# A recurrent trunk with product-key experts: prompt activations turned, and expert gates built from high and low halves

## The reference, cut to what matters

```
q = x @ w_q                                     # 8 heads, two halves of 128
s1, s2 = q_half1 @ keys1.T, q_half2 @ keys2.T   # 128 scores each
top16 of each, top16 of their 256 sums -> 16 (i, j) per head, gates = softmax
act[t, e] = gelu(x[t] . u[e])
out[t]    = sum over the 128 chosen e = (i, j) of gate * act[t, e] * v[e]
```

## Time and profile before

| | us |
|---|---|
| median of 3 runs | 5470.12 |
| the profiled execution | 5478.42 |
| its span, first to last instruction | 5476.7 |
| TensorE busy in the span | 5146.4 |
| VectorE busy | 2764.4 |
| ScalarE busy | 1416.8 |

### The profile page before, as it was taken

How to read it: one execution, slowest core, us unless ns; L and a number is a source line. 1 busy time by engine, 2 the same in 40 slices (tenths; PEclk the granted TensorE clock), 3 DMA queues, 4 the chain that set the end, 5 groups by cost and what they waited for, 6 DMA issues and landing times.

```text
span 5476.7 us, 70249 instructions
## 1 busy us (share of the span) xinstructions
PE 5146.4 (94%) x30167; PEld 4571.0 (83%) x30167; DVE 2764.4 (50%) x4785; ACT 1416.8 (26%) x1532; POOL 1495.3 (27%) x839
## 2 busy tenths in 40 slices
PE   5999779999999989999799999899999999999997
PEld 3767679999999978888566678889999999878886
DVE  2162668914434056666455541389524342266666
ACT  0110022223444222222222222112234443222222
POOL 0020222332222265542011110123322222465431
PEclk7969999999999999999799999999999999999999
DMA  7141022334444478886210011112334444588873
GB/s 292 63 166 58 20 77 82 121 118 154 154 157 158 164 258 304 303 303 249 84 39 32 31 47 43 47 62 108 123 130 156 155 161 148 198 314 300 296 295 135
DMA packets 295262, 835.85 MB, mean 153 GB/s; under 512 B 23922, under 2 KB 157298, under 8 KB 242726
## 3 DMA queue, kind: packets, MB, share of 16 engines
q1 hardware_dynamic: 91680, 520.91, 25.8%
q10 hardware_dynamic: 158216, 176.07, 9.3%
q0 software_dynamic: 45056, 134.38, 7.1%
HBM read 674.40 MB, written 156.80 MB: 152 GB/s over the span
## 4 chain that ended last, share of the span: by engine, by line
PE 89%; DVE 5%; POOL 2%; ACT 1%; issue 1%; DMA 1%; SPq 0%; DVEq 0%; ACTq 0%; POOLq 0%
PE PS L584 20%; PE PS L585 20%; PE PS L586 20%; PE PS L635 4%; PE PS L706 3%; PE PS L429 3%; PE PS L819 3%; PE PS L797 3%; PE PS L489 3%; PE PS L781 2%; POOL A L1837 1%; PE PS L576 1%; DVE EP L1338 1%; DMA ring<-in_w_mod 1%; PE PS L703 1%
## 5 line engine op out<-in xcount | busy, mean ns | idle before, releaser
L584 PE MATMUL PS<-hH,wH 128*128 128x320 f32 x4608 | 1439.5, 312 | 29.5 <-DVE hL L1106 28.4
L585 PE MATMUL PS<-hL,wH 128*128 128x320 f32 x4608 | 1425.5, 309 | 0.0
L586 PE MATMUL PS<-hH,wL 128*128 128x320 f32 x4608 | 1425.3, 309 | 0.0
L1826 POOL TENSOR_TENSOR wL<-raw,wH 128x2048 fp32r<-128x2048 f32 x144 | 667.9, 4639 | 1660.8 <-ACT wH L1560 1660.8
L584 PEld LDWEIGHTS PS<-hH,wH 128*128 128x128 f32 x4608 | 867.0, 188 | 30.7 <-issue 29.2
L585 PEld LDWEIGHTS PS<-hL,wH 128*128 128x128 f32 x4608 | 867.0, 188 | 0.0
L586 PEld LDWEIGHTS PS<-hH,wL 128*128 128x128 f32 x4608 | 866.2, 188 | 0.0
L1560 ACT ACTIVATE wH<-raw 128x2048 fp32r<-128x2048 f32 x272 | 520.3, 1914 | 1111.9 <-PE PS L586 1052.4
L586 PE MATMUL PS<-wH,WL 128*128 128x512 f32 x2048 | 803.7, 392 | 0.0
L1213 DVE TENSOR_TENSOR wL<-raw,wH 128x2048 fp32r<-128x2048 f32 x128 | 293.3, 2292 | 461.4 <-ACT wH L1560 461.4
L1845 POOL DMA_INDIRECT ubuf<-in_v,idxV x256 | 352.3, 1376 | 579.7 <-DVE acc L1225 536.2
(11 more groups left out here) (331 smaller groups left out, 6566.4 us busy)
## 6 DMA issues: line engine op xcount, KB each, us to landing
raw<-in_u SPq DMA_DIRECT2D x128, 1024.0 KB, 4.8
raw<-in_v SPq DMA_DIRECT2D x128, 1024.0 KB, 4.9
expert_acts<-abuf ACTq DMA_DIRECT2D x128, 640.0 KB, 2.9
expert_gates<-wide ACTq DMA_DIRECT2D x64, 1024.0 KB, 5.1
wide<-expert_acts SPq DMA_DIRECT2D x64, 1024.0 KB, 5.8
ring<-in_w_mod SPq DMA_DIRECT2D x48, 1024.0 KB, 9.0
wide<-expert_gates SPq DMA_DIRECT2D x16, 2048.0 KB, 11.7
gb<-expert_gates SPq DMA_DIRECT2D x16, 2048.0 KB, 12.1
```

The costliest lines, as they stand in the source:

```text
L584: nc.tensor.matmul(out, lhsH, rhsH, start=start, stop=False)
L585: nc.tensor.matmul(out, lhsH, rhsL, start=False, stop=False)
L586: return nc.tensor.matmul(out, lhsL, rhsH, start=False, stop=stop)
L1826: G.tensor_tensor(wL[:, n % NSPLIT, :], raw[:, n % NRAW, :], wH[:, n % NSPLIT, :].bitcast(f32), ALU.subtract).then_inc(lo_u, 1)
```

## The change

**Activations.** In `act_block` only the sample's 512 tokens are still made with the weights of `u` stationary: 8 x 3 = 24 matmuls of 512 columns a block, into one PSUM bank. The prompt's 128 tokens are turned: once a pair, after the second block, the tokens (`hH`, `hL`) are the stationary operand and the 256 experts of the pair the moving one: 24 matmuls of 256 columns into bank 2. They have a gelu, a buffer (`abuf0`) and a tensor in memory (`A0d`, token-major) of their own, stored every four pairs; `Ad` now holds the sample alone. `fetch_act` gathers from `A0d`; the index arithmetic on VectorE gets shorter.

**Gates.** The gates are split in a high and a low half (`gH`, `gP`). The one-hots are `f32r`, and the second is multiplied by either half, so a group has four VectorE operations of 128x1024 instead of three. A build is cut in two, `build(q, 0)` and `build(q, 1)`, of four tokens: four `f32r` matmuls of 256 columns, high and low side by side. The first stands in the middle of the block's 24 products, the second after its end (after the prompt's products, where the block has them). ScalarE copies the high part of four tokens to `gst` (`gate_half`), then VectorE adds the low part from PSUM to it in place (`gates_out`), and only that addition raises `g_evac`.

**The order on VectorE** is now: both one-hot groups 0 and 1, then for each q: addition (q, 0), the two comparisons of group q+1, addition (q, 1), the two multiplications of group q+1.

The core of the diff:

```diff
+    A0d = nc.dram_tensor("prompt_acts", [P, N_KEYS * N_KEYS], f32, kind="Internal").ap()
-    Ad = nc.dram_tensor("expert_acts", [NBLK, P, JB, T], f32, kind="Internal").ap()
+    Ad = nc.dram_tensor("expert_acts", [NBLK, P, JB, DEC], f32, kind="Internal").ap()
-    acts = Ad.rearrange("b p j (t o) -> (b p j t) o", o=1)
+    acts = A0d.rearrange("t (e o) -> (t e) o", o=1)
...
-    hots_ = wide[:, 4096:8192].rearrange("p (s c t n) -> p s c t n", s=2, c=2, t=8)
+    hots_ = wideR[:, 4096:10240].rearrange("p (s c t n) -> p s c t n", s=2, c=3, t=8)
+    gP = PS[:, 5:7, :]
+    gates_ = PS[:, 3:5, :].rearrange("p b (t c j) -> p c (b t) j", t=2, c=2)
...
-                    done(feature_major_split(slot, b % 2, b % 2), ("a", l, b))
+                    for half in range(2):
+                        for k in range(4 * half, 4 * half + 4):
+                            w = slice(k * SLICE + (b % 2) * P, k * SLICE + (b % 2 + 1) * P)
+                            last = split_products(PS[:, b % 2, :], wH[:, slot, w], wL[:, slot, w], hH[:, k, P:T], hL[:, k, P:T],
+                                                  k == 0, k == KD - 1)
+                        if half == 0 and build_group is not None:
+                            build(build_group, 0)
+                    done(last, ("a", l, b))
+                    if b % 2 == 1:
+                        if l * 64 + b // 2 >= 1:
+                            pe.wait_ge(act0_gelu, l * 64 + b // 2)
+                        for k in range(KD):
+                            w = slice(k * SLICE, (k + 1) * SLICE)
+                            last = split_products(PS[:, 2, 0:SLICE], hH[:, k, 0:P], hL[:, k, 0:P], wH[:, slot, w], wL[:, slot, w],
+                                                  k == 0, k == KD - 1)
+                        done(last, ("a0", l, b // 2))
+                    if build_group is not None:
+                        build(build_group, 1)
...
-                def build(q):
-                    pe.wait_ge(hot_ready, l * NGRP + q + 1)
-                    if q:
-                        pe.wait_ge(g_evac, l * NGRP + q)
-                    for tk in range(8):
-                        last = nc.tensor.matmul(PS[:, 4 + tk // 4, (tk % 4) * P:(tk % 4 + 1) * P], hots_[:, q % 2, 0, tk, :],
-                                                hots_[:, q % 2, 1, tk, :], start=True, stop=True)
+                def build(q, c):
+                    if c == 0:
+                        pe.wait_ge(hot_ready, l * NGRP + q + 1)
+                    if q or c:
+                        pe.wait_ge(g_evac, 2 * (l * NGRP + q) + c)
+                    for tk in range(4):
+                        last = nc.tensor.matmul(PS[:, 3 + tk // 2, (tk % 2) * 2 * P:(tk % 2 + 1) * 2 * P].rearrange("p (c j) -> p c j", c=2),
+                                                hots_[:, q % 2, 0, 4 * c + tk, :], hots_[:, q % 2, 1:3, 4 * c + tk, :], start=True, stop=True)
...
+                def gates_out(q, c):
+                    ve.wait_ge(g_high, 2 * (l * NGRP + q) + c + 1)
+                    first = (q % 2) * 8 + 4 * c
+                    out = gst[:, q // 2 % 2, :, first:first + 4].rearrange("p i t -> p t i")
+                    V.tensor_tensor(out, out, gates_[:, 1], ALU.add).then_inc(g_evac, 1)
+
+                for q in range(2):
+                    hots(q, 0)
+                    hots(q, 1)
                 for q in range(NGRP):
-                    hots(q)
+                    gates_out(q, 0)
+                    if 1 <= q < NGRP - 1:
+                        hots(q + 1, 0)
+                    gates_out(q, 1)
+                    if 1 <= q < NGRP - 1:
+                        hots(q + 1, 1)
...
+                def gate_half(q, c):
+                    s, first = q // 2 % 2, (q % 2) * 8 + 4 * c
+                    act.wait_ge(products, at["g", l, q, c])
+                    S.activation(gst[:, s, :, first:first + 4].rearrange("p i t -> p t i"), gates_[:, 0], ACT.Copy).then_inc(g_high, 1)
```

More of the change, by code:

```diff
@@ L249, in trunk @@
     WL1 = sb("WL1", [P, JV, DEC], f32r, scope=pv)
-    sb("v_pad", [P, 82 * KB], scope=pv)
+    sb("v_pad", [P, 80 * KB], scope=pv)
+    acc0 = sb("acc0", [P, D], scope=pv)
+    ubuf0 = sb("ubuf0", [P, D], scope=pv)
     WL0 = sb("WL0", [P, JV, DEC], f32r, scope=pv)
-    acc0 = sb("acc0", [P, D], scope=pv)
-    ubuf = sb("ubuf", [P, NGAT, D], scope=pv)
+    ubuf1 = sb("ubuf1", [P, NGAT - 1, D], scope=pv)
+    ubuf = [ubuf0[:]] + [ubuf1[:, i, :] for i in range(NGAT - 1)]
     pv.close()
@@ new lines, in act_block @@
+                    if build_group is not None:
[8 more added lines that the diff above has]
+                                                hots_[:, q % 2, 0, 4 * c + tk, :], hots_[:, q % 2, 1:3, 4 * c + tk, :], start=True, stop=True)
+                    done(last, ("g", l, q, c))
@@ L1180, in peer @@
                     ve.wait_ge(products, at["hk", l, t])
-                    V.tensor_copy(hkT[:, :, (t - 1) * P:t * P], PS[:, 4 + t % 2, 0:2 * P].rearrange("p (c t) -> p c t", c=2)).then_inc(hk_evac, 1)
+                    V.tensor_copy(hkT[:, :, (t - 1) * P:t * P], PS[:, 3 + t % 2, 0:2 * P].rearrange("p (c t) -> p c t", c=2)).then_inc(hk_evac, 1)
                 ve.wait_ge(hk_evac, l * 4 + 4)
[L1183 to L1187, removed]
+                link(V.tensor_copy(gH[:], gP[:, 0, :]))
@@ L1188, in hots @@
+                link(V.tensor_tensor(gP[:, 1, :], gP[:, 0, :], gH[:].bitcast(f32), ALU.subtract))
+                link(V.tensor_copy(gP[:, 0, :], gH[:].bitcast(f32)))
+                def hots(q, half):
                     ts = slice(8 * q, 8 * q + 8)
                     io = iotaP.unsqueeze(1).broadcast_to([P, 8, N_KEYS])
-                    do(V.tensor_tensor(hots_[:, q % 2, 0], io, bc(hkT[:, 0, ts], N_KEYS), ALU.is_equal))
-                    link(V.tensor_tensor(hots_[:, q % 2, 1], io, bc(hkT[:, 1, ts], N_KEYS), ALU.is_equal))
@@ L1192, in hots @@
-                    V.tensor_tensor(hots_[:, q % 2, 1], hots_[:, q % 2, 1], bc(gT[:, ts], N_KEYS), ALU.mult).then_inc(hot_ready, 1)
-                for q in range(NGRP):
-                    hots(q)
+                    one = hots_[:, q % 2, 2].bitcast(f32)
+                    if half == 0:
+                        if q >= 2:
+                            ve.wait_ge(products, at["g", l, q - 2, 1])
+                        do(V.tensor_tensor(hots_[:, q % 2, 0], io, bc(hkT[:, 0, ts], N_KEYS), ALU.is_equal))
+                        do(V.tensor_tensor(hots_[:, q % 2, 2], io, bc(hkT[:, 1, ts], N_KEYS), ALU.is_equal))
+                    else:
+                        settle()
+                        link(V.tensor_tensor(hots_[:, q % 2, 1], one, bc(gP[:, 0, ts], N_KEYS), ALU.mult))
+                        V.tensor_tensor(hots_[:, q % 2, 2], one, bc(gP[:, 1, ts], N_KEYS), ALU.mult).then_inc(hot_ready, 1)
@@ L1594, in peer @@
                         high(8 + pr + 1)
+                    q = b - B0
+                    if 0 <= q < NGRP:
+                        gate_half(q, 0)
                     act.wait_ge(products, at["a", l, b])
@@ L1597, in peer @@
                         act.wait_ge(a_stored[pr % 2], 16 * (l * 32 + pr // 2))
-                    S.activation(abuf[:, pr % 2, half, :].rearrange("p (a t) -> p a t", a=2), PS[:, 2 * half:2 * half + 2, 0:HT], ACT.Gelu).then_inc(act_gelu, 1)
+                    S.activation(abuf[:, pr % 2, half, :], PS[:, half, :], ACT.Gelu).then_inc(act_gelu, 1)
                     if half == 1:
@@ L1832, in peer @@
                     pool.wait_ge(a_stored[half], 16 * 32 * (l + 1))
-                pool.wait_ge(products, at["a", l, N_KEYS - 1])
+                    pool.wait_ge(a0_stored[half], 16 * 8 * (l + 1))
+                pool.wait_ge(products, at["a0", l, 63])
                 pool.wait_ge(hot_ready, NGRP * (l + 1))
@@ L1936, in act_load @@
                         else:
-                            sp.wait_ge(products, at["g", l, NGRP - 1])
+                            sp.wait_ge(products, at["g", l, NGRP - 1, 1])
                             for half in range(2):
@@ L1949, in gate_load @@
                         elif b == 1:
-                            sp.wait_ge(products, at["a", l, N_KEYS - 1])
+                            sp.wait_ge(products, at["a0", l, 63])
                         else:
```

92 lines of the change are left out of this document (45 added, 47 removed).

## The result

The changed kernel takes 5750.0 us (median of 4 runs, 5742.22 to 5774.34), the kernel before 5469.5 on the same chip: ratio 1.0514, 95% interval 1.0496 to 1.0532, so 5.1% slower. Forecast were 5677 and a range of 5585 to 5790. The profiled execution took 5756.35 us.

What follows compares the result with a forecast made beforehand. TensorE's own work was taken to bound the build stage. Chain +216, build start +4 and products -13 gave +207 on the profiled 5478.4, so 5685.4, or 5677 us for a median; range 5585 to 5790.

Steps and rivals of the forecast that it cites:

- What bounded the kernel: Gate-build stage, blocks 48 to 111: TensorE's own work sets the time, 8.83 us a block with a build.
- the wait that took over: Before each build's first half, TensorE waits for VectorE's multiplications: some 126 times, 2.0 to 2.9 us each, some 330 us.
- Products: TensorE's products in pairs without builds: 14.03 us before, 13.83 after, -13 us over 64 pairs.
- Rival 4: TensorE's 256-column matmuls come every 0.146 us, bound by weight loads: +106, 5783 us; chance 0.06.
- The chain's links: Copy, addition and multiplications between two builds: TensorE stands 2.47 and 2.83 us, a pair takes 21.03, +216 us.
- The price of the stride: VectorE's addition of 512 elements 16 floats apart: 1.22 us, against 0.69 contiguous.
- Rivals 1 and 2: VectorE's addition: stride costs nothing, 5593 us, chance 0.23; or is paid twice (1.75 us), 5778 us, chance 0.07.
- The start of the build: First build pair of each layer: TensorE stands about 7.3 us instead of 5.3, +4 us in all.
- The clock near 1.00: Build stage: TensorE's granted clock stays near full despite its waits.
- main case: Whole kernel: chain wait added, addition at 1.22 us, clock near 1.00; 5677 us, chance 0.47.
- a rival with 0.11: Build stage: TensorE's clock at the 1.2 GHz level 18% of the time, +86, 5763 us; chance 0.11.
- The end of the stage: Prompt's last store and gathers before the value stage: no change, with 10 us either way a layer.

Runs made afterwards that it cites:

- e1: Changed kernel with only VectorE's order altered: next group's two multiplications after the first addition, comparisons of the group after that behind the second; 5423.7 us.
- e5: Changed kernel with only the prompt's turned activation products kept, and gates built as in the kernel before; 5437.0 us, ratio 0.9940.
- e6: Changed kernel with added, unused VectorE additions and ScalarE copies of 512 elements at several strides; 5759.8 us in its one run.
- e4: Changed kernel with 16 more unused 256-column matmuls ahead of the first half of each build from group 2 on; 5616.9 us, ratio 1.0270.
- e7: Changed kernel with its order, but gate copy and addition write contiguously, which changes what is computed; 5504.3 us, ratio 1.0066.
- e3: Changed kernel with all four one-hot operations of the next group between the two additions, nothing behind the second; 5635.7 us, ratio 1.0300.

## Why the prediction was right

- **What bounded the kernel, and the wait that took over**: right. The named wait (L1216 before the first half of each build) came 126 times, as forecast, 1.9 to 2.2 us each, 248 us in all where I had 2.0 to 2.9 and some 330. e1 shows it is the order, not the amount of work. VectorE is busy 61% of the stage (302.63 of 500 us), not 70%, since the stage got longer than forecast and its operations are shorter.
- **Products**: right. Forecast 13.83 us a pair without builds, measured 13.78; 256-column products 0.1197 apart against 0.1185. -19 us in place of -13, and e5 gives -33 for the turned products over all 128 pairs. Rival 4 falls.
- **The chain's links**: right in kind, too long in sum. From the end of the block's products to the next build the trace has 5.24 us (1332.60 to 1337.84) where I had 5.69. The addition took 1.09 for 1.22, the multiplications 2.38 for 2.50, the wake-ups 0.02 to 0.04 where I took 0.05 and 0.17. ScalarE's copy was 1.05 for 1.07. In even blocks the first addition and the comparisons bind as said, but shorter too. At full clock a pair is 20.1 us for 21.03: +159 in place of +216.
- **The price of the stride**: near (1083 ns for 1.22 us), and it was right to go by ScalarE's row. Rivals 1 and 2 fall. The cache-line rule of the Trainium skill (SBUF — State Buffer, Door 1: The DMA port swizzle), which asks for at least two hits to a 16-byte line, pointed the right way: in e6 floats 2 apart, two to a line, cost nothing (689 ns) and floats 4 apart, one to a line, 1106. The formula of the Trainium skill (VectorE: DVE Perf Modes, The TRN2 errata) holds for the contiguous 689 ns and not for the strided 1083. What the Trainium skill says of strides stands in another section (VectorE: DVE Perf Modes, Mode 1× (REGULAR) — the baseline), and says that they work, not at what rate; I read more into it.
- **The start of the build** (+4): right in sign, small. In the first pair TensorE stands 4.07 and 0.66 us, where a pair stands about 3.9 later on: +0.9 a layer in place of +2.
- **The failed step: the clock.** "The clock near 1.00" was my main case, and a fall a rival with 0.11. It fell in 53 of 60 pairs. My reason against it was misread: of the gaps in the window of the earlier trace rows that I compared with, only one was long (5.03 us), and the others were under 0.5, so that window said nothing of repeated standings of 2 us. That its 18% is near the 22% measured is chance. The rival's price was too low as well: I let 18% of the time at the low level cost 6%, since I took the chain to be hidden under the slower products. But the low stretches lie on the products that follow a standing, where TensorE has work, so each microsecond of them loses about half of one: 0.22 x 22.47 / 2 = 2.5 us a pair, measured 2.33. I put it at +86; the trace has +149 and e4 gave back 133.
- **The end of the stage** at nothing: right. The gathers begin at 2067.62, 12.5 us after the last gelu of the prompt (2055.08), where it was 12.9.

The two misses are of opposite sign: 57 us too much for the chain, 149 left out for the clock. The forecast was 73 us low for their sum and the smaller terms. That it came so near is in part luck: with the clock full, as in my main case, the same chain takes 5616.9 us (e4), 60 under the forecast, and only the clock that I had given 0.11 carried the time past it. The way of the change and its wait were foreseen, the second half of the loss was not.

## What to carry to other kernels

When a hand-over between two engines gets a second half, write down what stands behind it in each queue: here the order of VectorE's queue alone was worth 326 us, with the same operations. Work for the next group goes ahead of the wait for this one's end, one group further ahead if the buffers allow. Price a standing of TensorE with what the clock does afterwards, and once one wait is gone, look at the moves that were worth nothing before.

## What the hardware showed that I had not expected

- **Standing of 2 us, twice a pair, was enough to lose the clock.** TensorE stood 1.9 to 2.2 us at a time (once 2.5) in the steady stage, and the granted clock was at the 1.2 GHz level for 22% of it. With 1.1 to 1.4 us at a time, once 1.7 (e7), it never went there, with some 2.3 and 0.8 in turn (e3) for 12%. Each fall cost 1.5 to 1.6 us (pairs of 20.1, 21.7, 23.2). Lengths between 1.7 and 1.9 us did not occur.
- **Useless products can pay**: 16 to a block in e4 took 133 us off, by keeping the clock up.
- **A float32 operand of 512 on VectorE costs nothing more 2 floats apart and 0.4 to 0.6 us more from 4 floats on**, once for read and write together (689 contiguous; 689, 1106, 1217, 1107, 1256 ns at 2, 4, 8, 16, 32); ScalarE's write is alike (622 contiguous; 673, 1117, 1231, 1102 at 2, 4, 8, 16). Three floats apart was not tried. Why 8 and 32 are dearer than 4 and 16 was not tried.
